# Row sums in the attentions, the router under the update, latents by block: one edit to a six-layer float32 kernel

## What is computed

```python
for layer in range(2):
    sh1, sc1, g1, sh2, sc2, g2 = split(silu(c) @ w_mod[layer] + b_mod[layer], 6)
    if layer == 0:                                       # attention A
        h = rmsnorm(x, a_norm_g) * (1 + sc1) + sh1
        mix = forgetting_attention(h, a_w_in, a_b_f, a_w_o)
    else:                                                # attention B
        h = rmsnorm(x, b_norm_g) * (1 + sc1) + sh1
        q = (rmsnorm(h @ b_w_dq, b_q_norm_g) @ b_w_uq)   # 768 -> 16 heads of 64 + 32 (rotated)
        mix = attend(q, shared_kv) @ b_w_o
    x = x + g1 * mix
    h = rmsnorm(x, ffn_norm_g[layer]) * (1 + sc2) + sh2
    scores = sigmoid(h @ router_w)                       # 16 experts in 4 groups
    # best group by its two best biased scores, the two best experts in it, weights normalised
    x = x + g2 * sum_over_experts(weight * ((silu(h @ w_gate) * (h @ w_up)) @ w_down))
    if layer == 0:
        h = rmsnorm(x, kv_norm_g) * (1 + sc_kv) + sh_kv
        c_kv, k_rope = split(h @ kv_w_down, [256])       # 1024 -> 256 + 32
        shared_kv = rmsnorm(c_kv, kv_latent_g) @ kv_w_up, rope(k_rope)      # 256 -> 2048
```

## Time and profile before

| | |
|---|---|
| median of 3 runs | 2652.74 us (2651.41 to 2655.47) |
| profiled execution | 2658.39 us, span 2656.6 us |
| PE, DVE, ACT, POOL busy | 93%, 64%, 50%, 3% of the span |
| HBM | 533.5 MB read, 202 GB/s over the span |
| chain that ended last | PE 64%, DVE 15%, DMA 10%, ACT 6%, issue 3% |

### The profile page before, as it was taken

The page is one execution under the profiler, slowest core; times in us unless marked ns, Lnnn a source line. Parts: engine busy times, 40 slices in busy tenths (PEclk is TensorE's granted clock), DMA queues, the critical chain, the costliest instruction groups (busy, mean ns, idle before and its releaser), DMA issues.

```text
span 2656.6 us, 31418 instructions
## 1 busy us (share of the span) xinstructions
PE 2474.7 (93%) x12658; PEld 2088.2 (79%) x12658; DVE 1705.8 (64%) x1536; ACT 1326.6 (50%) x1818; POOL 91.9 (3%) x121
## 2 busy tenths in 40 slices
PE   4988999998887999999999999899997999999999
PEld 3877777787777777778878888788886888987887
DVE  5757788787657777776544555645556555744555
ACT  3554777444554656643444444544445544444443
POOL 1000000100000000000000000100001000000000
PEclk8997999999998999999999999999999999999999
DMA  8713999984613978873644595335542455563553
GB/s 283 253 53 127 340 352 347 342 309 136 242 48 135 328 270 306 308 283 118 206 158 145 180 260 193 112 127 190 190 158 96 159 193 190 169 201 117 185 190 127
DMA packets 231296, 539.80 MB, mean 203 GB/s; under 512 B 21072, under 2 KB 29808, under 8 KB 231152
## 3 DMA queue, kind: packets, MB, share of 16 engines
q1 hardware_dynamic: 208992, 471.82, 51.0%
q0 software_dynamic: 15520, 59.77, 6.4%
q10 hardware_dynamic: 6640, 6.20, 1.2%
HBM read 533.54 MB, written 4.19 MB: 202 GB/s over the span
## 4 chain that ended last, share of the span: by engine, by line
PE 64%; DVE 15%; DMA 10%; ACT 6%; issue 3%; POOL 1%; SPq 1%; ACTq 0%; DVEq 0%
DVE w_low L2173 6%; PE pair L1008 6%; PE Y L1128 6%; PE Y L1130 6%; PE Y L1138 5%; PE pair L1051 4%; PE pair L1045 4%; PE pair L1046 4%; DMA raw<-in_exp_w_down 4%; DMA raw<-in_exp_w_gate 3%; PE pair L1016 3%; ACT w_high L1717 3%; PE pair L978 2%; PE pair L980 2%; PE pair L986 2%
## 5 line engine op out<-in xcount | busy, mean ns | idle before, releaser
L2173 DVE TENSOR_TENSOR w_low<-raw,w_high 128x2048 fp32r<-128x2048 f32 (+3 forms) x456 | 1021.4, 2246 | 583.7 <-ACT w_high L1717 581.6
L1717 ACT ACTIVATE w_high<-raw 128x1024 fp32r<-128x1024 f32 (+3 forms) x912 | 912.0, 1038 | 742.6 <-PE Y L1138 203.1
L1045 PE MATMUL pair<-w_high,hT 128*128 128x512 f32 (+1 forms) x612 | 240.7, 394 | 9.5 <-DVE hT L2229 5.2
L1046 PE MATMUL pair<-w_high,hT 128*128 128x512 f32 (+1 forms) x612 | 239.2, 391 | 0.0
L1128 PE MATMUL Y<-w_high,gated_high 128*128 128x512 f32 x528 | 205.8, 390 | 0.3 <-ACT w_high L1717 0.3
L1130 PE MATMUL Y<-w_high,gated_low 128*128 128x512 f32 x528 | 205.8, 390 | 0.0
L1008 PE MATMUL pair<-hT,w_high 128*128 128x512 f32 x768 | 183.0, 390 | 2.3 <-DVE work L2598 2.3
L1008 PEld LDWEIGHTS pair<-hT,w_high 128*128 128x128 f32 x768 | 142.5, 188 | 31.6 <-DVE work L2598 2.7
L1051 PE MATMUL pair<-w_low,hT 128*128 128x512 f32 (+1 forms) x612 | 152.5, 389 | 6.2 <-DVE w_low L2173 6.2
L1377 PE MATMUL pair<-w_high,rounded 128*128 128x512 f32 x384 | 154.8, 403 | 2.7 <-DVE gated_low L2498 2.7
L1378 PE MATMUL pair<-w_high,rounded 128*128 128x512 f32 x384 | 152.4, 397 | 0.0
(11 more groups left out here) (378 smaller groups left out, 4066.6 us busy)
## 6 DMA issues: line engine op xcount, KB each, us to landing
raw<-in_exp_w_gate SPq DMA_DIRECT2D x128, 512.0 KB, 4.5
raw<-in_exp_w_up SPq DMA_DIRECT2D x128, 512.0 KB, 4.8
raw<-in_exp_w_down SPq DMA_DIRECT2D x128, 512.0 KB, 4.6
raw<-in_w_up SPq DMA_DIRECT2D x128, 512.0 KB, 4.7
raw<-in_w_down SPq DMA_DIRECT2D x128, 512.0 KB, 4.3
work<-in_w_mod POOLq DMA_DIRECT2D x48, 1024.0 KB, 7.5
raw<-in_ret_w_in SPq DMA_DIRECT2D x96, 512.0 KB, 4.7
raw<-in_ret_w_out SPq DMA_DIRECT2D x32, 512.0 KB, 4.0
```

What stands on the lines that cost most here:

```text
L1045: nc.tensor.matmul(ps[:, b, 0:n], in_high[:, k0 + kk, bs], high[:, k, :], start=(kk == 0), stop=False)
L1046: nc.tensor.matmul(ps[:, b, 0:n], in_low[:, k0 + kk, bs], high[:, k, :], start=False, stop=False)
L1717: nc.scalar.activation(w_high[:, s % HIGH, part], raw[:, s % RAW, part], ACT.Copy).then_inc(high_ready, 1)
L2173: V.tensor_tensor(w_low[:, s % HIGH, 0:n], part, w_high[:, s % HIGH, 0:n].bitcast(F32), ALU.subtract).then_inc(low_ready, 1)
```

## The change

1. The row sums of modulations 8 and 9 (24 and 25) run inside attention A (B): two steps after each of the eight rounds. Their weights go to two areas that share their place with `gated_high` and `gated_low`, and POOL loads them before the attention.
2. PE multiplies the shift with the router's weights, now plain float32, in 8 products, right behind the output product, then both modulations in one use. x is turned bank by bank as the update's blocks come; DVE copies banks 0 and 1, ACT banks 2 and 3 into `turned_x`, and 16 float32 products with `router_w` times the gain (`router_g`) give the logits before the rows' scale. The thin products, their copy and the splitting of x into `hT` are gone here.
3. The low part of the rows comes after the selection; the first two gathers do their high parts before it. ACT and DVE take the first experts' pieces between the gathers. The heavy windows' split stands behind the first two experts' products. The tables of Sigmoid and Silu are loaded ahead of use by a one-column activation.
4. The latents are turned bank by bank; ACT scales one block at a time and DVE splits the keys' input two blocks at a time. `kv_up` is one chunk of two pieces of 128 x 2048. The queries' latent is turned into Y, its parts by pairs of blocks, and half a row sum moves behind the scaling of the queries' latent.

The diff, cut to its core (what is done for layer 1 repeats layer 0):

```diff
+        with nc.sbuf_tensor("gated_raw", [P, 2, 2048], F32) as gated_raw:
+            pass
...
+        gated_areas = [gated_raw[:, i].rearrange("p (k n) -> p k n", k=4) for i in range(2)]
+        mod_areas = {"a": areas_of(7168, 9216), "out_a": gated_areas, "moe0": areas_of(4096, 6144, 8192),
+                     "b": areas_of(8192, 16384), "out_b": gated_areas, "moe1": areas_of(4096, 6144)}
...
-            wait_full(pool, plan.att_a.scores[7])
+            wait_mod(pool, STAGES["a"][-1], 8)
...
-            load_mods((21,))
+            load_mod(21, 0)
             inverse_rms(plan.cq_stat)
+            load_mod(21, 1)
             load_mods((22, 23))
-            wait_full(pool, plan.att_b.scores[7])
+            wait_full(pool, plan.dq[1])
+            wait_mod(pool, STAGES["b"][-1], 8)
             load_mods(STAGES["out_b"])
...
+                wait_free(pe, m.router)
+                pe.wait_ge(later_loaded, 16 * N_LATER)
                 for k in range(KD):
                     at = MOD[m.nth] + SH2 + k
-                    shift = mod[:, at:at + 1].to_broadcast([P, P])
-                    nc.tensor.matmul(Y[:, 1536:1536 + EXPERTS], shift, thin_high[:, 1, k, :].bitcast(F32), start=(k == 0), stop=False)
-                    last = nc.tensor.matmul(Y[:, 1536:1536 + EXPERTS], shift, thin_low[:, 1, k, :].bitcast(F32),
-                                            start=False, stop=(k == KD - 1))
+                    last = nc.tensor.matmul(pair(m.router)[:, 512:512 + EXPERTS], mod[:, at:at + 1].to_broadcast([P, P]),
+                                            router_w[:, k, :], start=(k == 0), stop=(k == KD - 1))
                 last.then_inc(shift_done, 1)
+
+            def route_product(m):
+
+                blocks = [k for bank in range(4) for k in (bank, bank + 4)]
+                pe.wait_ge(router_ready, m.nth + 1)
+                for i, k in enumerate(blocks):
+                    if i % 2 == 0:
+                        pe.wait_ge(x_lower_copied if k < 2 else x_upper_copied, 2 * m.nth + k % 2 + 1)
+                    for b in range(TB):
+                        last = nc.tensor.matmul(pair(m.router)[:, b * EXPERTS:(b + 1) * EXPERTS],
+                                                turned_x[:, norm_at[k] + b * P:norm_at[k] + (b + 1) * P], router_g[:, k, :],
+                                                start=(i == 0 and b == 0), stop=(i == KD - 1 and b == TB - 1))
+                last.then_inc(fill_done, 1)
...
+            def modulations(ms, use):
+                wait_free(pe, use)
+                for i, m in enumerate(ms):
+                    last = mod_product(m, pair(use)[:, 4 * i:4 * i + 4])
+                last.then_inc(fill_done, 1)
...
+                for j in range(2):
+                    wait_free(pe, m.gather[j])
+                    light(j, xn_high, True)
+                pe.wait_ge(xn_low_made, m.nth + 1)
+                for j in range(2):
+                    light(j, xn_low, False).then_inc(fill_done, 1)
+                for j in range(2, KD // 2):
...
-                other_half = norm(m.norm, lambda: shift_product(m))
-                thin_product(m.router, 1, m.nth + 1, other_half)
+                turn_x(m.norm)
+                route_product(m)
                 keep_busy(8)
                 place_tokens(m)
-                keep_busy(8)
+                keep_busy(10)
                 gather_tokens(m)
...
+            shift_product(plan.moe0)
+            modulations(*plan.out_a_mods)
             experts(plan.moe0)
...
+            pe.wait_ge(scaled, TB * lt.scaled + 1)
+            for bank in range(2):
+                turn_latent(0, bank)
+                turn_latent(0, bank + 4)
+            pe.wait_ge(scaled, TB * (lt.scaled + 1))
+            for bank in range(4):
                 for b in range(TB):
-                    pe.wait_ge(scaled, TB * lt.scaled + b + 1)
-                    for k in range(4 * j, 4 * j + 4):
-                        last = nc.tensor.transpose(Y[:, k * S + b * P:k * S + (b + 1) * P], xn[:, b, k * P:(k + 1) * P], ident)
+                    if b or bank >= 2:
+                        turn_latent(b, bank)
+                        last = turn_latent(b, bank + 4)
                 last.then_inc(latent_turned, 1)
...
+            def kv_product(j):
+
+                use = plan.kv_up[j]
+                ps, ns = tokpair(pair(use)[:, :]), slice(512 * j, 512 * (j + 1))
+                wait_free(pe, use)
+                for k in range(2):
+                    s = 2 * plan.kv_piece + k
+                    high, low = w_high[:, s % HIGH, ns], w_low[:, s % HIGH, ns]
+                    wait_high(s, j // 2)
+                    for b in range(TB):
+                        bs = slice(b * P, (b + 1) * P)
+                        nc.tensor.matmul(ps[:, b, :], hT_high[:, k, bs], high, start=(k == 0), stop=False)
+                        nc.tensor.matmul(ps[:, b, :], hT_low[:, k, bs], high, start=False, stop=False)
+                    wait_low(s)
+                    for b in range(TB):
+                        last = nc.tensor.matmul(ps[:, b, :], hT_high[:, k, b * P:(b + 1) * P], low, start=False, stop=(k == 1))
+                    if j == 3:
+                        last.then_inc(piece_done, 1)
+                if j < 3:
+                    last.then_inc(fill_done, 1)
+
+            token_product(plan.kv_down, KD, KV_RANK + ROPE, inputs=for_kv, block_ready=kv_input)
+            token_product(plan.dq[0], inputs=for_b, block_ready=q_input)
...
-                se.wait_ge(ffn_gain, m.nth + 1)
-                norm(m.norm, gain)
-                copy_thin(m.router, m.nth + 1)
+                nc.scalar.activation(lam[:, 6:7], minus_half[:, 0:1], ACT.Sigmoid)
+                norm_squares(m.norm, tokpair(qT_area))
+                for bank in (2, 3):
+                    bs = slice(512 * bank, 512 * (bank + 1))
+                    se.wait_ge(norm_turned, m.norm.turn + bank + 1)
+                    nc.scalar.activation(turned_x[:, bs], Y[:, bs], ACT.Copy).then_inc(x_upper_copied, 1)
                 se.wait_ge(logits_ready, m.nth + 1)
                 nc.scalar.activation(route[:, 0, :], route[:, 0, :], ACT.Sigmoid).then_inc(emptied[m.router.u % 2], 1)
                 se.wait_ge(scaled, TB * (m.norm.scaled + 1))
                 nc.scalar.activation(xn_high, xn, ACT.Copy).then_inc(xn_high_made, 1)
+                nc.scalar.activation(lam[:, 7:8], minus_half[:, 0:1], ACT.Silu)
...
-                    last.then_inc(tmp_made, 1)
-                feed(2 * m.gate[0] + HIGH)
+                    last.then_inc(emptied[use.u % 2], 1)
+                    if j:
+                        feed(2 * m.gate[0] + j)
...
-                    se.wait_ge(latent_turned, j + 1)
-                    for i in range(4):
-                        k = 4 * j + i
-                        last = nc.scalar.activation(quads_of(tmp, j)[:, i, :], Y[:, k * S:(k + 1) * S], ACT.Identity,
-                                                    bias=mod[:, shift + k:shift + k + 1], scale=g[:, k:k + 1])
-                    last.then_inc(hT_high_made, 1)
+                for k in range(KD):
+                    se.wait_ge(latent_turned, k % 4 + 1)
+                    nc.scalar.activation(tmp[:, S * k:S * (k + 1)], norm_ps[k], ACT.Identity, bias=mod[:, shift + k:shift + k + 1],
+                                         scale=g[:, k:k + 1]).then_inc(hT_high_made, 1)
...
+                    for m in mods[n // 4:n // 4 + 1]:
+                        mod_steps(m, range(2 * (n % 4), 2 * (n % 4) + 2))
...
+                ve.wait_ge(xn_high_made, m.nth + 1)
+                V.tensor_tensor(xn_low, xn, xn_high.bitcast(F32), ALU.subtract).then_inc(xn_low_made, 1)
...
+                V.tensor_tensor(router_g[:], router_w[:], spread(gain[:, :], 2, EXPERTS), ALU.mult).then_inc(router_ready, 1)
+                ve.wait_ge(shift_done, m.nth + 1)
+                link(V.tensor_copy(shift_row[:], pair(m.router)[:, 512:512 + EXPERTS]))
+                for bank in range(2):
+                    bs = slice(512 * bank, 512 * (bank + 1))
+                    ve.wait_ge(norm_turned, m.norm.turn + bank + 1)
+                    last = V.tensor_copy(turned_x[:, bs], Y[:, bs])
+                    last.then_inc(x_lower_copied, 1)
                 scale_rows(m.norm)
...
+                def heavy_parts(j):
+                    ve.wait_ge(tmp_made, 2 * m.nth + 1 + j)
...
-            for n, _ in plan.out_a_mods:
-                mod_rows(n)
             update(plan.att_a.wo[1], 0, ahead=plan.att_a.ahead)
-            for mod_use in plan.out_a_mods:
-                mod_cols(mod_use)
+            mods_taken_together(*plan.out_a_mods)
...
+            for k in range(0, KD, 2):
+                latent_inputs(0, k, 2)
+            latent_inputs(1, 0, 4)
             feed(2 * c + 3)
-            latent_inputs(3)
+            latent_inputs(1, 4, 4)
             feed(2 * c + 4)
...
-            mod_rows(20)
```

(31 more changed lines are left out.)

210 lines of the change are left out of this document (111 added, 99 removed).

## The result

The changed kernel's median is 2613.1 us (four runs, 2606.7 to 2618.5) against 2652.1 for the kernel before, a ratio of 0.9851 (95% interval 0.9821 to 0.9881). Run again as after_again it gave 2607.9 and 0.9831 (0.9804 to 0.9857). So it is 39 to 45 us faster, where 34 were forecast; the profiled execution has a span of 2615.9 us instead of 2656.6, 40.7 less.

A forecast was written before the change was run, and what follows sets the result against it. With PE busy 93% of the span, the small stages between large products, where PE idles or runs slow, were taken as the bound. A 11.3, B 7.9 and latents 15 sum to 34.2 us: 2652.7 - 34 = 2619, range 2605 to 2638.

The forecast's parts named there:

- part 1: Row sums moved into the attention rounds: two rounds 8.4 us, costing +3.4 us in A and +2.6 in B.
- The rival that they pay in full: Row sums in the attentions: every step delays the chain, 24.4 us instead of 6.0, so 2637; chance 0.10.
- Part 2: Output product to logits: PE becomes the bound at 14.2 us, gaining 13.2 in A and 9.0 in B.
- rival "clock holds": Output product to logits: PE stays at 2.4 GHz, 9.0 us; 2 x 5.2 more gained, 2609; chance 0.14.
- Part 3: Routing and gathering up to the first experts: an earlier start gains 1.5 us in each place (0 to 4).
- Part 4: Latents: first products 4.0 us sooner, up products without their waits; 15 us gained (5 to 18).
- The sum: Whole kernel: A 11.3, B 7.9, latents 15, together 34.2 us gained, so 2619 us.
- rival that the clock falls in the attentions: Attention rounds: longer rounds leave PE emptier, clock falls, 48 us more instead of 6.0, 2661; chance 0.03.

The follow-up runs named there:

- sums_late: Changed kernel with the row sums moved to where DVE stood idle (none after rounds 0 to 3); 2603.8 us, ratio 0.9819 to the kernel before.
- latents_only: The kernel before with only item 4 of the change, the latents' part; 2631.7 us, ratio 0.9916 to the kernel before.

## Why the prediction was right

**What bounds the kernel, part 1.** Right. The sums cost 2.9 us in A's rounds 0 to 5 and 2.3 to 2.5 in B's (3.4 and 2.6 forecast), and sums_late takes them out again. That A's output product ended 3.3 us later in the first profile, where 3.4 were forecast, is partly luck: in after_again it ended only 0.5 later, with the same cost in the rounds, since that execution began its rounds 0.9 us earlier and the kernel before lost 1.4 us to the clock at the start of the product. Two rounds at 8.25 and 7.99 (8.4 worked out). The rival that they pay in full fell.

**Part 2.** Right in the mechanism: PE is the bound and each term is in the timeline (1.7 + 2.2 + 3.4 + 6.9 = 14.2 with the clock falling 3 us behind the product, 14.2 forecast too). What the prediction lacked is that this way is not one time but a spread: 10.6 to 14.8 in 14 stretches, mean 13.3, so that the first profile met 14.2 to 0.1 us was luck. The way before had a spread too, 23.2 and 27.4 in B in two traces, and the 9.0 forecast for B was taken from the shorter. The rival "clock holds" (9.0) is what some executions come close to, in part. The sentence of the Trainium skill (TensorE: Matmul & The Clock Gate, "Why this matters for your kernels") that lays drops to idle gaps between bursts was not borne out here: in these stretches PE was busy throughout at 0.50.

**Part 3.** This is the term that was mis-sized: 1.5 us in each place, by the argument that the light experts run at the pace of the stream and only hand an earlier start on. The pace itself changed: the split that moved behind the first products had stood in front of the low parts that free the stream's slots. Two units take 35.0 us on average in the ten traces with the deferral and 39.9 in the three without, 5 us less. Of these some are lost later where pieces land late: from the first gate product to the update behind the mixture, the kernels with the deferral took 372.9 to 386.2 us in A (mean 379.8, ten traces) and those without 381.8 to 383.9 (three); in B 372.5 to 381.9 (376.3) and 378.4 to 380.9 (379.7). So it is worth 3 us each on average, in two sets of traces that overlap. The way from the logits to the first gate product gives 1.8 in A and 1.3 in B (22.3 to 23.6 us in the ten; in before and latents_only 23.5 and 25.9 in A, 24.9 and 23.5 in B), which is close to the 1.5 forecast. Together it is about 5 instead of 1.5 (from the logits to the update 402.8 us in A and 399.2 in B on average, against 407.6 and 404.5 in before and latents_only), and with two traces on one side it is known to 2 or 3 us only. The forecast counted the earlier start alone and priced nothing for the deferral beyond it. The experts' order itself came 6.9 us behind the logits in both places (8.0 before), 1.0 us nearer where about 2 were forecast; in executions with the clock at 2.4 GHz there it came at 5.9.

**Part 4.** Right in the stretch: 14.4 to 15.5 us from the kernel before. The median of latents_only gained more than its trace explains. The start of the keys' latent came 2.1 to 2.6 us nearer to the update (2.5 forecast) and its end 2.7 to 3.5 (4.0); the rest came in the up products as worked out.

**The sum.** 34 forecast, 39 to 45 measured. The missing part is part 3, some 7 us in the two places together, as far as the scatter lets it be told. In the first pair of profiles it is also the clock at attention B's end, where the kernel before had two falls worth 4.1 us (64.7 us; latents_only has 60.6). Whether the kernel before has them in most executions isn't known from two traces. The rival that the clock falls in the attentions decided nothing: it fell there before and after, for 3.4 to 10.3 us at a time and at changing places, and in some executions not at all.

## What to carry to other kernels

When an instruction is moved off the chain, ask not only what waits for it but what it stood in front of on its own engine: here DVE's split delayed the freeing of the weight slots, and moving it shortened the first two experts' products by 5 us. Look for idle time of the engine in the trace after a change as well as before: one of the two row sums fits, half and half, into two idle pieces of 6 us that the new trace made easy to see. And where two profiles of one program differ by 3 us in a stretch, price a change in it by several traces.

## What the runs showed of the hardware

PE's clock fell from 2.4 to 1.2 GHz while PE had no gap, in all 14 stretches of small products (one column, sixteen columns, transposes of 128x128) from an output product to the logits, and in one of eight where products of 480 columns stood between them. In A of one and the same program the fall lasted 3.5 us in one execution and over 10 in another: after_again's router products took 3.8 us, the first profile's 6.9. A's experts took 386.2 and 378.8 us in those two traces. The difference is spread over many units: from the second unit's turning to the third's the slower one took 23.1 us, with ACT idle for 3.4 us until a down piece landed, but after_again took 21.7 there too.
